# Oldest chunk first or youngest chunk first: the order of three chunks in each step of a chunked recurrence

## The chip, the cores and the metric

The kernel runs on one core of one Trainium2 chip. The metric is device time in microseconds (us). Engines: PE is the matrix engine, PEld its weight loads, DVE the vector engine, ACT the scalar engine, POOL the general one, SP the one that issues most transfers here.

## The reference, cut to what matters

The reference runs two transformer layers over a prompt of 512 tokens and a sample of 64. The change touches one piece of layer 0, the RWKV-7 token mixer: a matrix state per head (8 heads, 64 x 64) is carried from token to token,

```
def step(state, inp):
    r_t, w_t, k_t, v_t, a_t, bb_t = inp
    sa = jnp.einsum('bhij,bhj->bhi', state, a_t)
    state = state * w_t[:, :, None, :] + sa[..., None] * bb_t[:, :, None, :] + v_t[..., None] * k_t[:, :, None, :]
    return state, jnp.einsum('bhij,bhj->bhi', state, r_t)
```

and each head's output is then layer-normalised, given a bonus term and gated. The prompt starts from a zero state, the sample from a state that is an input.

## The kernel before, in words

The kernel does not go token by token. It cuts the 576 tokens into 9 chunks of 64 (chunk 8 is the sample) and writes each chunk's part of the recurrence as small matrix products, 64 x 64 blocks for 8 heads at a time. A chunk passes through 18 stages, `k` = 0 to 17:

- 0 and 1 make the products of keys and queries inside the chunk; 2 to 12 invert a triangular matrix by products and additions; none of these needs the state.
- 13, 14 and 15 are the chunk's turn on the carried state `ST`. Behind product 15, DVE adds to the state and scales it (L1217, L1218), and goes on with the layer norm of the output: mean, centred value, variance.
- 16 has no product: POOL takes the inverse root (L111), DVE scales the block with it (L1193).
- 17 turns the block back on PE (L1093); DVE applies gain and bias (L1232, four instructions) and adds and gates (L1239, L1240).

A stage is a group of products by PE into one or both PSUM banks of the chunk's lane, and then copies by ACT (L1179) or sums by DVE out of them. Only when these are done may PE begin the lane's next stage: it waits on the lane's signal `taken`. There are three lanes (own banks, own work tiles), and chunk `c` uses lane `c % 3`, so chunk `c + 3` starts in the lane that chunk `c` leaves.

Chunks start 6 steps apart (`LAG`). In step `tau`, chunk `c` is at stage `k = tau - 6 * c`, so in steps 12 to 53 three chunks are under way, at `r`, `r + 6` and `r + 12` with `r = tau % 6`. I call six such steps a round; there are seven. Chunk 8 has in addition, ahead of its own products from step 54 on, the first tile of the output projection (`first_tile`, L1262), which fills PE while few chunks are left.

Every engine's instructions run in the order in which the program lists them; a wait holds everything behind it on that engine. That order is the list `turns`, sorted by step. Within a step it goes by chunk, oldest first, with two exceptions that move output stages to the end of a step (17 on PE, 16 and 17 on DVE):

```
turns = [(tau, c, tau - LAG * c) for tau in range(LAG * last + NS) for c in range(NCH) if 0 <= tau - LAG * c < NS]
```

Which of DVE and ACT takes which stage: DVE takes 0, 1, 2 (four instructions, with a copy by ACT beside them), 4 (with ACT), 5 (with ACT), 7, 10, 11, 12, 15, 16, 17; ACT alone takes 3, 6, 8, 9, 13, 14.

Of the kernel before, what the change touches and what calls it, by code (L numbers as in the profile page):

```python
# [758 lines left out]
def rwkv(nc, io, sb, sig, bank, CST, BV, MIX, PC, lw, W2A, G2, IDN, wide, side, PA, PB, OC, OBT, X):  # L759
# [25 lines left out]
    with ExitStack() as s2:  # L785
# [28 lines left out]
        with nc.Block() as block:  # L814
            @block.gpsimd
            def _(pool):

                pool.wait_ge(cl.h, cl.at(16))
                for q in halves:
                    for dst, mask in ((MSI, maskSI.rearrange("p (a n) -> p a n", a=2)[q, :, q]), (M16, mask16[q, q]),  # L820
                                      (MO, maskO[q, q]), (M16L, mask16L[q, q])):
                        pool.tensor_copy(dst[q], mask).then_inc(mh.h, 1)
# [210 lines left out]
    with ExitStack() as s2:  # L1033
# [39 lines left out]
        def count(c, k):  # L1073

            return c // LANES * PRODUCTS + min(k, 16)
# [3 lines left out]
        turns = [(tau, c, tau - LAG * c) for tau in range(LAG * last + NS) for c in range(NCH) if 0 <= tau - LAG * c < NS]  # L1079
# [88 lines left out]
        def act_stage(act, c, k):  # L1168

            lane, w = c % LANES, work[c % LANES]  # L1170
            b = w.b
            copies = {2: [(w.Bt, v4(b[1]))], 3: [(w.D2, v4(b[0])), (w.D2T, v4(b[1]))], 4: [(w.D4T, v4(b[0]))],
                      5: [(w.D4, v4(b[0]))], 6: [(w.D8T, v4(b[0])), (w.Kt, v4(b[1]))],
                      8: [(w.WT, v4(b[1]))], 9: [(w.NT, v4(b[0]))],
                      13: [(TMP[:, :, :], v4(b[0]))], 14: [(SA, v4(b[1]))]}.get(k, [])
            if copies:
                act.wait_ge(made[lane].h, made[lane].at(count(c, k) + 1))
                for dst, src in copies:
                    ins = act.activation(dst, src, ACT.Copy)  # L1179
                ins.then_inc(taken[lane].h, 1 if k in (2, 4, 5) else 2)  # L1180
# [68 lines left out]
        def first_tile(pe, tau):  # L1249

            if tau == 54:
                for k in range(4):
                    m = pe.transpose(bank[6][:, k * P:(k + 1) * P], OC[:, 0, k * P:(k + 1) * P], ident)
                m.then_inc(ot.h, 1)
            for b, k in FIRST.get(tau, ()):
                if (b, k) == (0, 0):
                    pe.wait_ge(oc.h, oc.at(1))
                    pe.wait_ge(wl[0].h, wl[0].at(16))
                if (b, k) == (0, 4):
                    pe.wait_ge(wl[1].h, wl[1].at(32))  # L1260
                lhs = OCT[:, k * P:(k + 1) * P] if k < 4 else OBT[:, k - 4, 0:P]
                m = pe.matmul(bank[7 - b], lhs, first_out[k][:, b * 512:(b + 1) * 512], start=(k == 0), stop=(k == 7))  # L1262
                if k == 7:
                    m.then_inc(fo.h, 1)
# [3 lines left out]
        with nc.Block() as block:  # L1268
            @block.sync
            def _(sp):  # L1270
                wv = io["l0_w_out"].rearrange("(k p) n -> p k n", p=P)

                def through(c):
                    sp.wait_ge(made[c % LANES].h, made[c % LANES].at(count(c, 15) + 1))

                sp.dma_start(FO[:, 0:4, :], wv[:, 0:4, :]).then_inc(wl[0].h, 16)
                sp.dma_start(FO[:, 4:7, :], wv[:, 4:7, :]).then_inc(wl[1].h, 16)
                sp.dma_start(first_out[7], wv[:, 7, :]).then_inc(wl[1].h, 16)
                through(6)
                sp.dma_start(XF[:, 2560:3584], io["x_prompt"][0, 0:P, :]).then_inc(xf.h, 16)  # L1280
                sp.wait_ge(st_sig.h, st_sig.at(last))
                sp.dma_start(io["out_b_wkv_p"], ST[:, :, :]).then_inc(stored.h, 16)

                through(last - 1)
                sp.wait_ge(stored.h, stored.at(16))
                sp.dma_start(ST[:, :, :], io["wkv_t"]).then_inc(loaded.h, 16)
                sp.wait_ge(st_sig.h, st_sig.at(NCH))
                sp.dma_start(io["out_b_wkv_s"], ST[:, :, :]).then_inc(stored.h, 16)
                sp.wait_ge(stored.h, stored.at(32))

            @block.tensor
            def _(pe):
                for tau, c, k in sorted(turns, key=lambda turn: (turn[0], turn[2] == 17)):
                    if c == last:
                        first_tile(pe, tau)
                    pe_stage(pe, c, k)

            @block.scalar
            def _(act):
                for tau, c, k in turns:  # L1300
                    act_stage(act, c, k)
                    if (tau, c) == (55, last):
                        act.wait_ge(ot.h, ot.at(1))
                        act.activation(OCT, bank[6], ACT.Copy).then_inc(oc.h, 1)

            @block.gpsimd
            def _(pool):
                pool.memset(ST[:, :, :], 0.0).then_inc(zs.h, 1)
                pool.memset(OBT[:, :, TOK:PADT], 0.0).then_inc(zs.h, 1)
                for c in range(NCH):  # L1310
                    roots.give(pool, c, ys[:, 1, :])

            @block.vector
            def _(dve):
                ch = Chain(dve, dve_chain)
                for tau, c, k in sorted(turns, key=lambda turn: (turn[0], turn[2] > 15)):
                    if (c, k) == (0, 15):
                        dve.wait_ge(zs.h, zs.at(2))
                    if (c, k) == (last, 15):
                        dve.wait_ge(loaded.h, loaded.at(16))  # L1320
                    dve_stage(dve, ch, c, k)
                dve_chain.end(ch.n)
# [1497 lines left out]
```

## Time and profile before

| what | value |
|---|---|
| time, median of 3 runs | 3630.05 us (3628.56 to 3630.25) |
| the profiled execution's own time | 3630.2 us |
| its span | 3628.3 us |
| busy shares over the span | PE 83%, DVE 71%, ACT 37%, POOL 40% |
| the recurrence, first product to last gating | 328.0 to 503.6 us |
| three chunks under way, first to last full round's state update | 366.91 to 460.00 us |

In the timeline a product stands as two instructions, so the `x8` of the program's listing is `x16` there; the length shown for the last one reaches past the moment at which the next group may begin. The busy shares are means over a kernel of many stages; the recurrence is a twentieth of the span. Behind it comes the long part that gathers expert rows from memory.

### The profile page before, as it was taken

To read this page: it belongs to the slowest core of one execution; us is meant where nothing else is said; L and a number is where in the kernel's file an instruction comes from. 1 tells how busy PE (TensorE), PEld (TensorE's weight loads), DVE (VectorE), ACT (ScalarE), POOL (GpSimd) and SP (SyncE) were. 2 spreads that over 40 slices of the span, in tenths; PEclk is the share of its full clock that TensorE was granted. 3 is DMA by queue.
4 is the path that set the end of the run, shared out by engine and by line. 5 is a ranking of instruction groups with operands and counts; after the bars stand their busy time and mean duration, and the time that the engine had idled before them with its cause. 6 is when DMAs were issued, how large, how long until landed. Compare 5 with 4: busy or idle time off the path is not lost. (4 is left out here: it accounts for less than half of the span.)

```text
span 3628.3 us, 38367 instructions
## 1 busy us (share of the span) xinstructions
PE 3009.7 (83%) x11628; PEld 1431.6 (39%) x11628; DVE 2588.6 (71%) x6361; ACT 1343.5 (37%) x4033; POOL 1434.6 (40%) x1241
## 2 busy tenths in 40 slices
PE   8997969887777778999898788988988877777777
PEld 5774854342223223434344333433434322233222
DVE  2675648876666667798978577999777666666664
ACT  3354213333333333336653332345633333333332
POOL 1200014544444445454345454543444444444443
PEclk9997989999999999999998999999999999999999
DMA  4101049999999999999899999999999999999998
GB/s 134 39 15 48 4 164 420 412 419 408 422 421 421 401 421 396 419 410 389 330 413 403 393 415 419 420 411 344 416 421 421 414 413 420 421 421 406 422 421 352
DMA packets 216573, 1293.40 MB, mean 356 GB/s; under 512 B 23600, under 2 KB 41008, under 8 KB 68784
## 3 DMA queue, kind: packets, MB, share of 16 engines
q0 software_dynamic: 165888, 1208.03, 81.1%
q1 hardware_dynamic: 50480, 82.93, 6.5%
q8 instruction: 92, 1.51, 0.2%
q14 instruction: 113, 0.93, 0.1%
HBM read 1286.49 MB, written 3.87 MB: 356 GB/s over the span
## 5 line engine op out<-in xcount | busy, mean ns | idle before, releaser
L1592 PE MATMUL banks<-ring,route 128*128 128x512 f32 (+1 forms) x4184 | 2020.9, 620 | 525.7 <-ACT route L1577 504.0
L1500 POOL DMA_INDIRECT ring<-in_uv,route x1152 | 1326.3, 1151 | 1683.2 <-PE banks L1592 1541.1
L1511 DVE SCALAR_TENSOR_TENSOR ring<-ring,XN 128x1024 f32<-128x1024 f32 x1152 | 1423.4, 1236 | 742.7 <-DMA ring<-in_uv,route 732.6
L1592 PEld LDWEIGHTS banks<-ring,route 128*128 128x128 f32 (+1 forms) x4184 | 741.8, 188 | 1637.0 <-issue 857.3
L1562 ACT ACTIVATE route<-route 128x2 f32<-128x2 f32 x576 | 117.3, 204 | 1836.5 <-DVE ring L1511 1836.1
L1577 ACT ACTIVATE route<-IDN,route 128x128 f32<-128x128 f32 x918 | 317.0, 387 | 4.3 <-PE banks L1592 3.4
L1567 ACT ACTIVATE route<-route 128x1 f32<-128x1 f32 x1152 | 276.7, 287 | 23.1
L1920 PE MATMUL banks<-own,QP 128*128 128x512 f32 (+1 forms) x400 | 178.3, 570 | 4.1 <-ACT QP L2011 2.7
L1562 ACT ACT_TABLE_LOAD x106 | 136.0, 1283 | 1.9
L1521 DVE SCALAR_TENSOR_TENSOR X<-ring,route,X 128x1024 f32<-128x1024 f32 x106 | 135.7, 1280 | 0.0
L1920 PEld LDWEIGHTS banks<-own,QP 128*128 128x128 f32 x400 | 77.2, 194 | 94.2 <-issue 83.9
L1511 DVE DVE_READ_ACCUMULATOR ring<-ring,XN 128x1 f32 x1152 | 94.4, 82 | 0.0
L1408 ACT ACT_TABLE_LOAD x71 | 91.1, 1283 | 1.3
L1980 PE MATMUL banks<-own 128*128 128x320 f32 (+1 forms) x256 | 72.6, 425 | 3.9 <-DMA own<-in_l_peer_wq 3.9
L1972 PE MATMUL banks<-own,QP 128*128 128x512 f32 x160 | 75.2, 595 | 0.7 <-DMA own<-in_l_w_out 0.7
L111 POOL TENSOR_TENSOR ys<-ys,IDN 128x4 f32<-128x4 f32 x9 | 9.1, 1008 | 162.1 <-DVE ys L1228 162.1
L507 PE MATMUL banks<-XT,ring 128*128 128x288 f32 x288 | 71.8, 406 | 0.0
L111 POOL TENSOR_TENSOR hs<-hs,IDN 128x8 f32<-128x8 f32 x12 | 26.6, 2220 | 112.7 <-DVE hs L736 112.7
L1980 PEld LDWEIGHTS banks<-own 128*128 128x128 f32 x256 | 48.9, 196 | 37.7 <-issue 27.7
L507 PEld LDWEIGHTS banks<-XT,ring 128*128 128x128 f32 x288 | 54.6, 190 | 17.5 <-issue 2.4
L2403 PE MATMUL banks<-own 128*128 128x448 f32 x128 | 53.6, 545 | 0.0
L1467 DVE TENSOR_TENSOR route<-route 128x512 f32<-128x512 f32 x72 | 49.5, 687 | 0.0
(450 smaller groups left out, 3082.0 us busy)
## 6 DMA issues: line engine op xcount, KB each, us to landing
ring<-in_uv,route POOLq DMA_INDIRECT x1152
own<-in_l_w_in SPq DMA_DIRECT2D x16, 1024.0 KB
own<-in_l_w_out SPq DMA_DIRECT2D x12, 1024.0 KB
own<-in_l_peer_wq SPq DMA_DIRECT2D x12, 1024.0 KB
X<-in_x_prompt SPq DMA_DIRECT2D x8, 512.0 KB, 7.7
ring<-in_l_w_in SPq DMA_DIRECT2D x4, 1024.0 KB, 9.8
ring<-in_l_peer_wq SPq DMA_DIRECT2D x2, 2048.0 KB, 12.0
own<-in_l_w_in SPq DMA_DIRECT2D x4, 656.0 KB
```

Of the source, the lines that this page charges most:

```text
L507: m = pe.matmul(bank[(NT + i) % 2][:, 0:HALF], W[HOMES[s]][:, k, w], XT[:, k, HALF * half:HALF * half + HALF], start=(k == 0), stop=(k == ...
L1408: act.activation(self.GX, self.BS, ACT.Exp, bias=self.NM, accum_out=self.GS[:, 0:1]).then_inc(self.exped.h, 1)
L1500: pool.indirect_dma_start(self.ring[:, s % RING, :], None, self.io[f"uv{of_slot(s)[0]}"], bass.IndirectOffsetOnAxis(ap=self.EI[:, g % 2, k ...
L1511: dve.scalar_tensor_tensor(u, u, 1.0, self.XN[:, of_slot(s)[1], :], ALU.mult, ALU.mult, accum_out=self.HD[:, g % 2, k:k + 1]).then_inc(sel ...
L1521: dve.scalar_tensor_tensor(x, self.ring[:, s % RING, D:], self.WG[:, g % 2, k:k + 1], x, ALU.mult, ALU.add).then_inc(self.v_vector.h, 1)
L1562: act.activation(self.HG[:, par, k:k + 2], self.HD[:, par, k:k + 2], ACT.Gelu).then_inc(self.gelus.h, 1)
L1567: act.activation(self.WG[:, par, k + i:k + i + 1], self.HG[:, par, k + i:k + i + 1], ACT.Copy, scale=self.GT[:, g % 3, k + i:k + i + 1]).t ...
L1577: act.activation(self.DG[:, n % 4, 0:cols], on, ACT.Copy, scale=self.WG[:, par, k + i:k + i + 1]).then_inc(self.diagonals.h, 1)
L1592: m = pe.matmul(self.bank[1 + half][0:n, :], self.DG[:, (V_TENSOR[s] - 1) % 4, 0:n], self.ring[:, s % RING, D + 512 * half:D + 512 * half ...
L1920: m = pe.matmul(out[:, 0:W.shape[2]], self.QP[:, self.tiles[i], k, :], W[:, k % HK, :], start=(k == 0), stop=(k == KD - 1))
L1972: m = pe.matmul(out, self.QP[:, self.tiles[i], k, :], W[:, k % HK, :], start=(k == 0), stop=(k == KD - 1))
L1980: m = pe.matmul(out[:, 0:self.width()], W[:, k % HK, i * P:i * P + P], self.XQ[:, k, 0:self.width()], start=(k == 0), stop=(k == KD - 1))
```

## The change

Each of PE, ACT and DVE now sorts its turns by stage as well, so within a step the chunk with the lowest stage, the youngest, comes first. Output stages stay last on PE and DVE. No instruction is added or removed, no tile, bank, transfer or lane changes.

```diff
             @block.tensor
             def _(pe):
-                for tau, c, k in sorted(turns, key=lambda turn: (turn[0], turn[2] == 17)):
+                for tau, c, k in sorted(turns, key=lambda turn: (turn[0], turn[2] == 17, turn[2])):
                     if c == last:
                         first_tile(pe, tau)
                     pe_stage(pe, c, k)
 
             @block.scalar
             def _(act):
-                for tau, c, k in turns:
+                for tau, c, k in sorted(turns, key=lambda turn: (turn[0], turn[2])):
                     act_stage(act, c, k)
...
             @block.vector
             def _(dve):
                 ch = Chain(dve, dve_chain)
-                for tau, c, k in sorted(turns, key=lambda turn: (turn[0], turn[2] > 15)):
+                for tau, c, k in sorted(turns, key=lambda turn: (turn[0], turn[2] > 15, turn[2])):
```

Three places in the round in which chunk 2 is the oldest (lane 2, `banks2`), chunk 3 the middle one (lane 0, `banks0`) and chunk 4 the youngest (lane 1, `banks1`); chunk 5 then follows chunk 2 in lane 2.

The first place is PE from the last step of the round into the next round. Before, the rows are stages 11 and 5, then 17 of chunk 2, then 12 of chunk 3, 6 of chunk 4 (two rows) and 0 of chunk 5:

```order
L1087 MATMUL banks0<-PA 64x64 x8
L1087 MATMUL banks1<-PB 64x64 x16
L1093 MATMUL banks2<-CST,PB 64x64 x8
L1087 MATMUL banks0<-PA 64x64 x8
L1087 MATMUL banks1<-PB 64x64 x8
L1093 MATMUL banks1<-CST,ring 64x64 x8
L1108 MATMUL banks2<-ring,own 64x128 x8
```

After the change the same stretch of PE reads 5, 11, 17, then 0, 6 (two rows), 12:

```order
L1087 MATMUL banks1<-PB 64x64 x16
L1087 MATMUL banks0<-PA 64x64 x8
L1093 MATMUL banks2<-CST,PB 64x64 x8
L1108 MATMUL banks2<-ring,own 64x128 x8
L1087 MATMUL banks1<-PB 64x64 x8
L1093 MATMUL banks1<-CST,ring 64x64 x8
L1087 MATMUL banks0<-PA 64x64 x8
```

Stage 0 of the new chunk (L1108) now stands directly behind stage 17 of the chunk that leaves the same lane; the stages 12 and 6 that stood between them come behind it.

The second place is PE from step 2 of the round into step 3. Before, the rows are 14 of chunk 2 and 8 of chunk 3, then 2 of chunk 4 (two rows), then the first rows of 15 of chunk 2:

```order
L1087 MATMUL banks2<-ring,PB 64x64 x8
L1093 MATMUL banks0<-CST,PA 64x64 x8
L1087 MATMUL banks1<-own,ring 64x64 x8
L1093 MATMUL banks1<-CST,own 64x64 x8
L1154 MATMUL banks2<-PB 64x64 x2
L1156 MATMUL banks2<-ring,PB 64x64 x2
```

After the change they are 2 (two rows), 8, 14, then 3 of chunk 4, 9 of chunk 3, and the first row of 15:

```order
L1087 MATMUL banks1<-own,ring 64x64 x8
L1093 MATMUL banks1<-CST,own 64x64 x8
L1093 MATMUL banks0<-CST,PA 64x64 x8
L1087 MATMUL banks2<-ring,PB 64x64 x8
L1087 MATMUL banks1<-PB 64x64 x16
L1087 MATMUL banks0<-PA,X 64x64 x8
L1154 MATMUL banks2<-PB 64x64 x2
```

Between stages 2 and 3 of the youngest chunk there stood the whole of stage 15 and stage 9; now stages 8 and 14 stand there.

The third place is PE behind stage 15. Before, the last row of 15 is followed by 9 and 3 of its own step, then by 10, 4 and 11:

```order
L1162 MATMUL banks2<-ring,PB 64x64 x2
L1087 MATMUL banks0<-PA,X 64x64 x8
L1087 MATMUL banks1<-PB 64x64 x16
L1087 MATMUL banks0<-PA 64x64 x8
L1087 MATMUL banks1<-PB 64x64 x16
L1087 MATMUL banks0<-PA 64x64 x8
```

After the change the last row of 15 is followed by 4 and 10, and then by 5 and 11:

```order
L1162 MATMUL banks2<-ring,PB 64x64 x2
L1087 MATMUL banks1<-PB 64x64 x16
L1087 MATMUL banks0<-PA 64x64 x8
L1087 MATMUL banks1<-PB 64x64 x16
L1087 MATMUL banks0<-PA 64x64 x8
```

Stages 9 and 3 have moved ahead of 15. On DVE the whole of 15 still comes ahead of the sums of 10 and 4, and these two have changed places.

## Rows read from the trace of the kernel before

**Rows 1.** Windows, two stretches of the recurrence: stretch, busy time by engine, granted clock, DMA, GB/s.

```profile
328.00:340.00 12.00, 7.89 (x96) 6.74 (x96) 3.08 (x6) 0.77 (x3) 0.56 (x2) 0.50 0.91 345
400.00:420.00 20.00, 18.66 (x569) 17.80 (x571) 14.38 (x38) 4.77 (x13) 2.02 (x2) 1.00 0.02 4
```

**Rows 2.** Timeline of DVE, the first state update with three chunks and the last.

```profile
366.91 0.42 DVE L1217 TENSOR_TENSOR STr<-banks,STr 128x256 f32<-128x256 f32 x1 [0.60 <-PE banks L1162]
...
460.00 0.42 DVE L1217 TENSOR_TENSOR STr<-banks,STr 128x256 f32<-128x256 f32 x1 [0.53 <-PE banks L1162]
```

**Rows 3.** Timeline of PE in one round: start, length, operation, count, [idle before <- releaser].

```profile
392.51 1.04 PE L1108 MATMUL banks<-ring 64*64 64x128 f32 x16
393.38 0.63 PE L1087 MATMUL banks<-ring,PB 64*64 64x64 f32 x16
...
394.93 0.63 PE L1093 MATMUL banks<-CST,own 64*64 64x64 f32 x16
395.39 0.28 PE L1154 MATMUL banks<-PB 64*64 64x64 f32 x4
...
397.73 0.63 PE L1087 MATMUL banks<-PA,X 64*64 64x64 f32 x16
398.19 1.10 PE L1087 MATMUL banks<-PB 64*64 64x64 f32 x32
399.13 0.63 PE L1087 MATMUL banks<-PA 64*64 64x64 f32 x16
400.05 1.15 PE L1087 MATMUL banks<-PB 64*64 64x64 f32 x32 [0.29 <-ACT PB L1179]
401.40 0.68 PE L1087 MATMUL banks<-PA 64*64 64x64 f32 x16 [0.20 <-DVE PA L1213]
...
402.85 0.63 PE L1093 MATMUL banks<-CST,PB 64*64 64x64 f32 x16
403.31 0.63 PE L1087 MATMUL banks<-PA 64*64 64x64 f32 x16
...
404.25 0.63 PE L1093 MATMUL banks<-CST,ring 64*64 64x64 f32 x16
405.14 1.09 PE L1108 MATMUL banks<-ring,own 64*64 64x128 f32 x16 [0.26 <-DVE PB L1232]
406.57 0.33 PE L1145 MATMUL banks<-STr,ring 64*64 64x64 f32 x4 [0.34 <-DVE PA L1215]
```

**Rows 4.** Timeline of DVE in the same round.

```profile
395.61 0.43 DVE L1202 TENSOR_TENSOR PB<-PB,own 128x256 f32<-128x256 f32 x1 [1.25 <-PE banks L1093]
...
396.99 0.43 DVE L1205 TENSOR_TENSOR PB<-banks,own 128x256 f32<-128x256 f32 x1
397.94 0.42 DVE L1217 TENSOR_TENSOR STr<-banks,STr 128x256 f32<-128x256 f32 x1 [0.53 <-PE banks L1162]
...
402.13 0.42 DVE L1193 TENSOR_TENSOR PB<-PB,ys 128x256 f32<-128x256 f32 x1 [0.46 <-POOL ys L111]
...
403.53 1.55 DVE L1232 TENSOR_SCALAR PB<-banks,BV 128x64 f32<-128x64 f32 x4
```

**Rows 5.** Timeline of PE in the later part: two waits for ACT.

```profile
1514.55 3.64 PE L1592 MATMUL banks<-ring,route 128*128 128x512 f32 x4 [1.91 <-ACT route L1577]
...
3399.65 2.84 PE L1592 MATMUL banks<-ring,route 128*128 128x512 f32 x6 [2.23 <-ACT route L1577]
```

**Rows 6.** Windows behind these waits, columns as in rows 1.

```profile
1514.50:1515.00 0.50, 0.45 (x1) 0.37 (x2) 0.00 (x0) 0.00 (x0) 0.44 (x1) 0.73 1.03 422
...
1518.00:1518.50 0.50, 0.50 (x3) 0.41 (x2) 0.26 (x2) 0.00 (x0) 0.03 (x1) 0.86 0.94 385
...
3402.00:3403.00 1.00, 1.00 (x4) 0.28 (x2) 0.71 (x1) 0.00 (x0) 0.84 (x1) 1.00 1.05 434
```

**Rows 7.** Timeline of SP and PE where the next part begins.

```profile
504.42 0.43 SPq L2542 DMA_DIRECT2D ring<-in_l_peer_wq  x1
...
514.94 1.40 PE L2614 MATMUL banks<-XN,ring 128*128 128x128 f32 x5 [2.70 <-DMA ring<-in_l_peer_wq]
```

## The prediction

> **What bounds the kernel now.** I read three views. The windows come first, to see which engine fills the recurrence: with three chunks under way PE is busy 18.66 of 20 us, DVE 14.38, ACT 4.77, at the full granted clock, and almost nothing is transferred [rows 1]. So PE's queue sets the pace, and what counts is the time in which PE stands still. Next the state updates on DVE, which give the length of a round: from 366.91 to 460.00 are six rounds, 15.51 us each [rows 2]. Last the timeline of PE and DVE in one round, to see where PE stands still and for whom [rows 3, 4].
>
> In rows 3 the time between the starts of two groups is what a group costs. A group of 8 products takes 0.46 us (402.85 to 403.31), a two-bank group of 16 takes 0.94 (398.19 to 399.13), a group with 128 columns 0.87 (392.51 to 393.38). What a start comes later than that is a stall. There are four in a round:
>
> - stage 0 at 405.14: 0.89 behind the group ahead of it, so a stall of 0.43. It waits for the four L1232 of the chunk that leaves its lane.
> - stage 13 at 406.57: 1.43 − 0.87 = 0.56. It waits for stage 12's sum, which on DVE stood behind L1239 and L1240.
> - stage 4 at 400.05: 0.92 − 0.46 = 0.46. It waits for ACT's two copies of stage 3.
> - stage 11 at 401.40: 1.35 − 0.94 = 0.41. It waits for stage 10's sum, which stood behind all of stage 15 on DVE.
>
> That is 1.86 us of 15.51. The carried state is not what sets the round: a state update starts at 397.94, and the next chunk's stage 13 takes it up at 406.57 [rows 3, 4]. Bringing the oldest chunk forward or back is therefore worth nothing in itself; only the cover behind each wait counts.
>
> **The change part by part.** Nothing is added or removed; the work of a round, 15.51 − 1.86 = 13.65 us of PE, stays. For each lane I ask how long its engine needs before the lane's next stage may begin, and what PE has to do meanwhile. From the end of a group's issue DVE starts 0.22 us later (394.93 + 0.46 = 395.39 to 395.61), and PE starts 0.06 us behind DVE's end (403.53 + 1.55 = 405.08 to 405.14) [rows 3, 4].
>
> First place, **stage 17 and stage 0 of one lane**. PE's 17 takes 0.46, DVE then needs 0.22 + 1.55 + 0.06 = 1.83 before stage 0 may start. Before, 12 and 6 lay between (0.46 + two groups of 0.46) and left 0.43 exposed. Now nothing lies between: PE stands still for 1.83, and behind it wait 6, 12 and all that follows. L1239 and L1240 now run beside stage 0's products (0.87 + 0.22 before DVE could use them), so they delay nothing. This meets chunks 3 to 8: six times.
>
> Second place, **stage 2 to stage 3 of the youngest**. DVE's four instructions run from 395.61 to 396.99 + 0.43 = 397.42; with the start and the way back 0.22 + 1.81 + 0.06 = 2.09 [rows 4]. Before, stages 15 and 9 covered it fully. Now 8 and 14 do, 0.92: a stall of 1.17, in each of seven rounds. 9 and 15 are late behind it.
>
> Third place, **behind stage 15**. From the end of its issue at 397.73 to the start that follows DVE's first free sum, 401.40, are 3.67 us [rows 3]. Before, 9, 3, 10 and 4 covered all but the stalls 0.46 and 0.41. Now DVE takes stage 4's sum first, an instruction of the same length, and PE has only 4 and 10 to do, 0.94 + 0.46 = 1.40: a stall of 2.27, seven times. 5, 11 and 17 wait behind it. Stage 17 itself also needs POOL's root and L1193, done at 402.13 + 0.42, 4.82 behind the end of 15's issue; PE comes to it at 3.67 + 0.94 + 0.46 = 5.07, so this stays hidden by 0.25 us, and costs at most that little if I am off.
>
> What goes away: stage 0's 0.43 six times, and the 0.56 (12 and 13 now have 1 and 7 between them, 0.87 + 0.46), the 0.46 (stage 15's 2.33 us now cover ACT's copies of 3) and the 0.41 seven times each. ACT's own order moves with PE's and nothing waits on it at either end: its work is 4.77 of 20 us [rows 1].
>
> The sum: 6 × 1.83 + 7 × (1.17 + 2.27) = 35.1 us come, 6 × 0.43 + 7 × (0.56 + 0.46 + 0.41) = 12.6 go, net 22.5 us. A full round becomes 15.51 − 1.86 + 5.27 = 18.9 us. Steps 0 to 11 and 54 to 65 get no term: with one or two chunks the two orders differ little, and at the end the first tile's products fill PE. Nothing behind the recurrence takes the delay up: the next part's first weights are asked for at 504.42, after the recurrence's end at 503.6, and PE waits for them at 514.94 [rows 7]; so the whole amount reaches the end.
>
> **The clock** is the part that no row of this stretch shows. At the third place PE now idles 2.27, does 1.86 of work (5, 11, 17) and idles 1.83 again; as the timeline counts idle time (the last product reaches 0.17 past its group's cost) these are 2.1 and 1.66. Elsewhere in this trace an idle time of 1.91 was followed by a fall of the granted clock, while one of 2.23 was not [rows 5, 6]. The fall: 0.73 in the half microsecond from 1514.50 means from about 1514.73; 0.86 in that from 1518.00 means until about 1518.14. That is 3.4 us at 1.2 instead of 2.4 GHz, so some 1.7 us lost where PE is the bound, as it is behind the first place (0, 6, 12, 1, 7, 13 follow without a stall). The bounds are nothing and one fall in each round, 7 × 1.7 = 11.9 us. Two waits close together, of lengths between which the rows are divided, make me take three falls in seven rounds: 5.1 us.
>
> The Trainium skill speaks against the change more strongly here: TensorE: Matmul & The Clock Gate, section "HAM oscillation — how this bites in real kernels", tells of bursts of products between waits that begin at the low clock each time and pay for it each time. By that rule the sum would be 22.5 + 11.9. The trace agrees with it at 1514.55 and not at 3399.65.
>
> **Rivals.**
> - The clock holds: 3630.2 + 22.5 = 3652.7. For it: rows 5's 2.23. 30%.
> - The clock falls in some rounds, the forecast: 3630.2 + 22.5 + 5.1 = 3657.8. 40%.
> - It falls in every round (this is the skill's rule): 3630.2 + 34.4 = 3664.6; twice in some, up to 3676. 15%.
> - PE stays at the low clock throughout, as from 328 to 340, when one chunk alone kept it busy 7.89 of 12 us at 0.50 [rows 1]: 13.65 us of work a round doubled is 27.3, and 7 × 11.8 make 3713. Against it: 6.6 us of unbroken work follow each first place. 3%.
> - The largest new wait is covered by something I don't see, say DVE doing stage 4's sum ahead of the layer norm's tail: then 7 × 2.27 fall out, and 3637 is left. Against it: the listing puts the sum behind all of 15, and DVE takes its instructions in order throughout rows 4. 6%.
> - Faster: only the four old stalls count. It would need the three waits (1.83, 2.09, 3.67) to be over before PE is through with the work that covers them (0, 0.92, 1.40), that is, from new stalls under 1.86 a round on the sign turns. With none of them 3630.2 − 12.6 = 3617.6. For it speaks that every lane still has two others to hide behind in a cycle of three; against it, that stage 15, the one long piece of PE, now stands beside two lanes whose waits are already over. 4%.
> - No change, because a later wait for a transfer takes the delay up: 3630. Rows 7 show no transfer under way that could. 2%.
>
> **How the numbers follow.** The forecast is the likeliest case, 3658 us; the profiled execution of before (3630.2) stands 0.15 us above the median of the runs, so I correct nothing. The range holds the first three cases but not the doubled falls: from 3645 (the 22.5 with a third of it wrong) to 3670 (a fall in each round and some 5 us more). Anything beyond 0.2%, 7.3 us, is about what a measurement can tell from no change. Slower takes the first five cases, 0.94; faster 0.04; within the bound 0.02.
>
> **What the changed profile would show.** The state updates on DVE 18.9 us apart, or up to 20.6 where the clock fell. Before stage 0 (L1108) an idle time of about 1.7 us released by L1232; before stage 3 about 1.0 released by L1205; before stage 5 about 2.1 released by L1207, the sum of stage 4. No wait of stage 13 for L1215, none of stage 4 for ACT. PE busy about 72% of these 20 us. The clock at 1.00, with dips to 0.50 of some 3.4 us behind the pair of waits. The recurrence would end near 531, and everything behind it would look as before. It would be wrong if updates stayed near 15.5 us apart, or if one of the three releasers were another engine.

## The result

| | before | changed |
|---|---|---|
| time, median of 4 runs each | 3629.31 us (3625.33 to 3630.25) | 3658.66 us (3657.25 to 3659.22) |
| ratio, 95% interval | | 1.008 (1.0069 to 1.0092) |
| the profiled execution's own time, span | 3630.2, 3628.3 us | 3659.11, 3657.2 us |
| recurrence, start of the first product to end of the last L1240 | 175.5 us | 206.2 us |
| one round, mean of six | 15.52 us | 20.37 us |

The change makes the kernel 29 us slower; the forecast was 3658 (3645 to 3670). The total is right and its two terms are not: the profile after and the first run below show that the stalls brought less than 22.5 us and the clock more than 5.1.

The windows of the changed kernel, for the stretches of [rows 1]: PE was busy 18.66 of the 20 us from 400, and is now busy 15.28; the granted clock, 1.00 before, has a mean of 0.91.

```profile
328.00:340.00 12.00, 7.63 (x96) 6.45 (x93) 3.08 (x6) 1.04 (x3) 0.26 (x2) 0.50 0.90 349
400.00:420.00 20.00, 15.28 (x436) 14.81 (x434) 10.78 (x27) 3.90 (x11) 1.01 (x1) 0.91 0.01 3
```

DVE's state updates of the changed kernel, at the start and the end of six rounds as in [rows 2], are 122.22 us apart, against 93.09 before.

```profile
367.58 0.42 DVE L1217 TENSOR_TENSOR STr<-banks,STr 128x256 f32<-128x256 f32 x1 [4.12 <-PE banks L1162]
...
489.80 0.42 DVE L1217 TENSOR_TENSOR STr<-banks,STr 128x256 f32<-128x256 f32 x1 [4.05 <-PE banks L1162]
```

PE's timeline in one round of the changed kernel, for [rows 3]:

```profile
402.56 0.63 PE L1087 MATMUL banks<-ring,PB 64*64 64x64 f32 x16
404.17 1.15 PE L1087 MATMUL banks<-PB 64*64 64x64 f32 x32 [0.97 <-DVE PB L1205]
...
408.88 0.63 PE L1087 MATMUL banks<-PA 64*64 64x64 f32 x16
411.61 1.68 PE L1087 MATMUL banks<-PB 64*64 64x64 f32 x32 [2.09 <-DVE PB L1207]
413.08 1.06 PE L1087 MATMUL banks<-PA 64*64 64x64 f32 x16
413.94 1.06 PE L1093 MATMUL banks<-CST,PB 64*64 64x64 f32 x16
416.66 1.09 PE L1108 MATMUL banks<-ring,own 64*64 64x128 f32 x16 [1.66 <-DVE PB L1232]
```

All three new stalls are there, with the releasers and the lengths that were forecast: stage 3 waits for stage 2 on DVE (404.17 − 402.56 − 0.46 = 1.15 us), stage 5 for stage 4's sum behind all of 15 (411.61 − 408.88 − 0.46 = 2.27), stage 0 for L1232 of the chunk that leaves its lane. What wasn't forecast stands between the last two: from the start of stage 11 to that of stage 17 it is 0.86 us, not 0.46. DVE's timeline has stage 4's sum (L1207), which starts at 411.14 behind the layer norm, and L1232, which reads stage 17:

```profile
411.14 0.42 DVE L1207 TENSOR_TENSOR PB<-banks,PB 128x256 f32<-128x256 f32 x1
...
415.05 1.55 DVE L1232 TENSOR_SCALAR PB<-banks,BV 128x64 f32<-128x64 f32 x4 [0.36 <-PE banks L1093]
```

The windows of the changed kernel around these stages, columns as in [rows 1], the granted clock last but two:

```profile
411.00:411.50 0.50, 0.00 (x0) 0.00 (x0) 0.47 (x4) 0.00 (x0) 0.19 (x1) 1.00 0.00 0
411.50:412.00 0.50, 0.39 (x12) 0.39 (x14) 0.39 (x2) 0.00 (x0) 0.50 (x1) 0.99 0.00 0
412.00:412.50 0.50, 0.50 (x16) 0.50 (x14) 0.15 (x1) 0.00 (x0) 0.32 (x1) 0.50 0.00 0
...
415.00:415.50 0.50, 0.00 (x1) 0.00 (x0) 0.41 (x2) 0.00 (x0) 0.00 (x0) 0.59 0.07 16
```

From about 411.99 to 415.41 PE has 1.2 instead of 2.4 GHz. By such windows the clock fell in each of the seven rounds (once for 6.8 us, else 3.4), each time right behind the stall that follows stage 15. The old stalls are gone: in the list of waits of PE in these rounds neither L1215 nor L1213 nor ACT's L1179 is left as a releaser, and stage 0's idle 0.26 [rows 3] has become the 1.66 above.

What follows the recurrence is only later [rows 7]: the weights asked for at 504.42 are now asked for at 534.79, and PE's first product with them starts 30.9 us later:

```profile
545.85 1.41 PE L2614 MATMUL banks<-XN,ring 128*128 128x128 f32 x5 [3.23 <-DMA ring<-in_l_peer_wq]
```

The whole execution is 28.9 us longer, so some 2 us come back in the 3100 us behind. Runs of before differ among themselves by more (3626 to 3633), and I didn't follow it.

### The profile page after: what moved, and what is told of

It reads as the page before. It is cut to its first block and busy times, and to the rows that moved or that the text cites. A ratio compares the mean times of both kernels' runs of the same rounds, so it can differ in the third digit from the quotient of the medians.

```text
span 3657.2 us, 38367 instructions
## 1 busy us (share of the span) xinstructions
PE 3022.9 (83%) x11628; PEld 1444.5 (39%) x11628; DVE 2586.2 (71%) x6361; ACT 1342.6 (37%) x4033; POOL 1439.3 (39%) x1241
## 5 line engine op out<-in xcount | busy, mean ns | idle before, releaser
L1087 PE MATMUL banks<-PB 64*64 64x64 f32 x1152 | 46.9, 235 | 17.5 <-DVE PB L1207 10.5
L1179 ACT ACTIVATE PB<-banks 128x256 f32<-128x256 f32 x63 | 22.6, 383 | 85.2 <-PE banks L1087 50.2
```

## The experiments

All ten in one table; the ratio is given where a kernel was timed in several runs, the rest were run once. "Length" and "round" are those of the first table, each from one profiled execution.

| run | time, us | ratio (95%) | length, us | round, us | clock in the rounds |
|---|---|---|---|---|---|
| e1_filled | 3648.2 | 1.005 (1.0035 to 1.0065) | 195.7 | 18.78 | 1.00 |
| e2_young_early | 3636.4 | 1.002 (1.001 to 1.0029) | 183.3 | 16.96 | 1.00 |
| e3_young_late | 3665.6 | 1.0096 (1.008 to 1.0111) | 214.4 | 20.57 | falls in each |
| e4_middle_first | 3626.9 | 0.9991 (0.9982 to 1.0001) | 173.6 | 15.05 | 1.00 |
| e5_act_old | 3662.7 | | 211.3 | 20.58 | falls in each |
| e6_young_end | 3625.0 | | 175.3 | 15.52 | 1.00 |
| e7_filled_lane | 3662.0 | | 207.7 | 20.30 | falls in each |
| e8_middle_end | 3627.4 | 0.9993 (0.9984 to 1.0002) | 172.7 | 15.05 | 1.00 |
| e9_half_filled | 3646.3 | | 195.3 | 18.79 | 1.00 |
| e10_filled_inverse | 3658.1 | | 206.0 | 20.34 | falls in each |

**The stalls without the clock.** The first run fills the longest stall of the changed kernel with products whose results nobody uses:

```diff
                     pe_stage(pe, c, k)
+                    if k == 10 and 12 <= tau < 54:
+                        for _ in range(2):
+                            pe.matmul(bank[6][:, :], ident, CST[:, 0:512], start=True, stop=True)
```

> The changed kernel with two extra products (128x512, into a bank that lies idle until step 54) on PE behind stage 10 in steps 12 to 53; their results are not used. By rows of the first tile two such products take 1.9 us, so they lie inside the stall of 2.27 behind stage 15 and shift nothing. Theory (the low clock behind that stall costs about 1.4 us a round on top of the stalls): the granted clock stays at 1.00, a round is 18.9 us instead of 20.4, the recurrence ends some 9 to 10 us earlier than in the changed kernel, the time is about 3649. Rival (the extra 1.4 us a round are not the clock, or the second stall of 1.66 drops it all the same): the round stays at 20.1 to 20.4, time 3657 to 3660. Third case: the extra products delay stages 5 and 11, and the time is above 3660.

PE does more work and the kernel is 10.5 us faster than the changed one. In its timeline of PE the extra products (L1299) lie in the stall, and stage 0 still waits, by 413.30 − 411.01 − 0.46 = 1.83 us (1.66 as idle time):

```profile
407.40 1.98 PE L1299 MATMUL banks<-CST,IDN 128*128 128x512 f32 x4
409.56 1.15 PE L1087 MATMUL banks<-PB 64*64 64x64 f32 x32 [0.18 <-DVE PB L1207]
...
411.01 0.63 PE L1093 MATMUL banks<-CST,PB 64*64 64x64 f32 x16
413.30 1.09 PE L1108 MATMUL banks<-ring,own 64*64 64x128 f32 x16 [1.66 <-DVE PB L1232]
```

Its windows show that the clock doesn't fall:

```profile
400.00:420.00 20.00, 17.12 (x476) 15.34 (x472) 11.63 (x30) 4.66 (x13) 1.01 (x1) 1.00 0.01 4
```

Its state updates, in DVE's timeline, are 112.66 us apart over six rounds:

```profile
368.56 0.42 DVE L1217 TENSOR_TENSOR STr<-banks,STr 128x256 f32<-128x256 f32 x1 [4.12 <-PE banks L1162]
...
481.22 0.42 DVE L1217 TENSOR_TENSOR STr<-banks,STr 128x256 f32<-128x256 f32 x1 [4.05 <-PE banks L1162]
```

So the two terms are parted. With the clock up the recurrence is 195.7 − 175.5 = 20.2 us longer than before: that is the stalls. The other 206.2 − 195.7 = 10.5 us are the clock, 1.5 a round.

**Each half of the round alone.** Both runs sort as below, with `turn[0] % 6 < 3` (e2) or `turn[0] % 6 > 2` (e3) as the condition `young`:

```diff
-                for tau, c, k in sorted(turns, key=lambda turn: (turn[0], turn[2] == 17)):
+                for tau, c, k in sorted(turns, key=lambda turn: (turn[0], turn[2] == 17, turn[2] if young else -turn[2])):
...
```

> Youngest first only in steps 0 to 2 of a round; steps 3 to 5 keep the order of before. Theory (a sum of covers): stage 0 directly behind 17 stalls 1.83 (before 0.43), stage 15 now comes directly behind stage 14 of its own lane and waits for ACT's copy, about 0.7, stage 13's 0.56 goes, those of 4 and 11 stay; a round of 15.51 + 1.40 + 0.7 - 0.56 = 17.1, time 3630 + 6 x 1.40 + 7 x 0.15 = 3639 to 3641 if the clock holds with a single idle time of 1.7 a round. Rival (any such wait drops the clock once a round): some 7 to 10 us more, 3647 to 3650.

The round is 16.96 us; the terms of the sum make 17.05, not 17.1. The clock holds. The time is 3 us under what was expected; the first update comes 1.25 us earlier behind the first product than before, and the rounds make under 1 of it. The timeline shows stage 0's stall and the one that this mixture adds, stage 15 (L1154) waiting for ACT's copy of 14:

```profile
406.73 1.09 PE L1108 MATMUL banks<-ring,own 64*64 64x128 f32 x16 [1.66 <-DVE PB L1232]
...
413.90 0.33 PE L1154 MATMUL banks<-PB,X 64*64 64x64 f32 x4 [0.54 <-ACT PB L1179]
```

> Youngest first only in steps 3 to 5; steps 0 to 2 keep the order of before. Theory: stage 3 comes directly behind stage 2 of its own lane, a stall of 2.09 us; behind stage 15 the stall of 2.27 is there as in the changed kernel; stages 4's 0.46 and 11's 0.41 go, 0's and 13's stay; a round of 15.51 + 2.09 + 2.27 - 0.87 = 19.0 with the full clock, time 3630 + 7 x 3.49 = 3654. The two idle times lie 5 us apart here, not 1.9. If it is the pair close together that drops the clock, it stays at 1.00 and the time is 3654; if the one idle time of 2.1 behind stage 15 does it, the clock falls in every round as in the changed kernel and the time is 3661 to 3666.

A round is 20.57 us: the 19.0 of the sum and 1.6 more, which I put down to the clock; no run has this order with the clock up. It falls, though no two of the long idle times stand close together (6.9 and 9.7 us lie between them), so the prediction's picture of a pair is not needed. But it doesn't fall where I expected either. Of the 38.9 us by which the recurrence is longer than before, 8.2 lie ahead of the first update; I didn't split them. Its timeline of PE, the idle 2.09 behind stage 15 and the 1.90 ahead of stage 3:

```profile
399.61 0.68 PE L1087 MATMUL banks<-PA 64*64 64x64 f32 x16 [2.09 <-DVE PA L1207]
...
411.18 1.15 PE L1087 MATMUL banks<-PB 64*64 64x64 f32 x32 [1.90 <-DVE PB L1205]
```

Its windows behind the one and the other: the first leaves the clock at 1.00, the second is followed by the fall.

```profile
400.00:400.50 0.50, 0.50 (x24) 0.50 (x22) 0.15 (x1) 0.00 (x0) 0.31 (x1) 1.00 0.00 0
...
412.00:412.50 0.50, 0.50 (x22) 0.50 (x20) 0.00 (x0) 0.12 (x1) 0.00 (x0) 0.83 0.00 0
```

**Which idle time drops the clock.** Three more kernels fill one stall each of the changed kernel, by products like those of the first run: behind stage 17 (e7: 512 and 384 columns), half of the one behind stage 15 (e9: 512 columns behind stage 10), and the one ahead of stage 3 (e10: 512 columns behind stage 14).

```diff
                     pe_stage(pe, c, k)
+                    if k == 14 and 12 <= tau < 54:
+                        pe.matmul(bank[6][:, 0:512], ident, CST[:, 0:512], start=True, stop=True)
```

> The changed kernel with two extra products (128x512 and 128x384, results not used) behind stage 17, in the stall ahead of stage 0; the stall behind stage 15 stays open. Theory (the idle time of 2.1 behind stage 15 is what drops the clock, with or without the one ahead of stage 0): the clock still falls to 0.50 in every round right behind it; stage 17 and the extra products then run at half rate and overrun their stall by about 1.5 us, round 20 to 22 us, time 3660 to 3672. Rival (the prediction's: the two idle times 1.9 apart drop it together): the clock stays at 1.00, the extra products (some 1.7 us at full rate) fit into the stall of 1.83, round 18.9, time about 3649.

> The changed kernel with one extra product (128x512, result not used) behind stage 10, which leaves some 1.2 us of the idle time behind stage 15 open; the idle times of 1.66 ahead of stage 0 and 0.97 ahead of stage 3 stay. Theory (an idle time of 2.1 there is what drops the clock, and 1.66 does not, as in the run with youngest first only in steps 0 to 2): clock at 1.00, round 18.8, time about 3649. Rival (the sum of the three idle times in a round decides, now about 3.8 instead of 4.7): the clock still falls in some rounds, which are then 20 us long, time 3653 to 3659.

> The changed kernel with one extra product (128x512, result not used) behind stage 14, which fills the idle time of 0.97 ahead of stage 3; those of 2.1 behind stage 15 and 1.66 ahead of stage 0 stay. Theory (the 2.1 behind stage 15 decides): the clock falls in every round, rounds of 20.1 to 20.4, time 3656 to 3662. Rival (idle time over the whole stretch from stage 2 to stage 5 decides, so that less of it ahead keeps the clock up): clock at 1.00, round 18.8, time about 3649.

With stage 0's stall filled (e7) the idle 2.1 stands as it was, by the timeline of PE:

```profile
410.19 1.80 PE L1087 MATMUL banks<-PB 64*64 64x64 f32 x32 [2.10 <-DVE PB L1207]
```

and the windows behind it show that the clock falls all the same:

```profile
410.50:411.00 0.50, 0.50 (x16) 0.50 (x14) 0.07 (x1) 0.00 (x0) 0.39 (x1) 0.50 0.00 0
```

With stage 3's filled (e10) the idle 2.1 stands, too, by the timeline:

```profile
412.71 1.79 PE L1087 MATMUL banks<-PB 64*64 64x64 f32 x32 [2.10 <-DVE PB L1207]
```

and the windows:

```profile
413.00:413.50 0.50, 0.50 (x16) 0.50 (x14) 0.05 (x1) 0.00 (x0) 0.42 (x1) 0.50 0.00 0
```

With half of the one behind stage 15 filled (e9) the timeline has 1.04 idle left:

```profile
407.88 1.15 PE L1087 MATMUL banks<-PB 64*64 64x64 f32 x32 [1.04 <-DVE PB L1207]
```

The clock then holds, by the windows, and the round is that of the full filling:

```profile
400.00:420.00 20.00, 15.89 (x460) 14.72 (x462) 11.15 (x28) 3.89 (x11) 1.01 (x1) 1.00 0.01 3
```

In the changed kernel, then, the idle 2.1 behind stage 15 is the cause, and neither of its neighbours is needed by itself; idle times of 1.66 and 0.97 drop nothing. Nor is it the sum of the idle times: e7 leaves 2.10 + 0.97 = 3.07 us of them in a round and the clock falls, e9 leaves 1.04 + 1.66 + 0.97 = 3.67 and it holds. Length alone isn't the rule, as e3 shows. In e7 the extra products overran their stall by less than 0.1 us, not by the 1.5 that I expected.

**ACT's order.** The changed kernel with the line of ACT as it was:

> The changed kernel with ACT's order of before; PE and DVE as changed. Theory of the prediction (ACT's order decides nothing, ACT is busy a fifth of the time and each of its copies has cover): rounds as in the changed kernel, 20.1 to 20.4 us, time 3656 to 3662. A sum of covers in finer steps says a little more: in step 2 ACT then copies 14 and 8 ahead of stage 2's block, done about 0.2 us after DVE's four instructions, so stage 3 starts 0.2 later and a round is 0.2 longer. Rival (the orders of PE and ACT must agree, or PE stands still for copies): a stall released by ACT of 0.5 us or more in each round, time above 3663.

The time lies between the two. In its list of waits (total, times, longest) stage 3 now waits for ACT, up to 1.1 us, where it waited 0.97 for DVE:

```profile
PE banks L1087 <- ACT PB L1179: 6.9, 7, 1.1
```

By the letter this is the rival's sign, a stall of over 0.5 us released by ACT, but it stands in the place of one that was there. A round is 0.2 longer; one of them has the low clock for 6.8 us, as in the changed kernel. In this one run the whole recurrence is 5 us longer: 2 ahead of the first update, 1.3 in the rounds, the rest behind them. So ACT's order is worth tenths of a microsecond in a round, a little more than the nothing that the prediction gave it, and it adds no stall of 0.5.

**The last steps.** The condition `young` is now `turn[0] > 53`:

> The order of before up to step 53, youngest first only in steps 54 to 65, where chunks 7 and 8 are left and the first tile fills PE. The prediction gave these steps no term; in the changed kernel the two intervals from the seventh state update on hold some 1.6 us less than its stalls and its clock make up. Theory (the new order gives this back there, since stage 9 of the last chunk and the first tile's products stand ahead of stage 15 instead of behind it): rounds of 15.5, and the recurrence ends 1 to 2 us earlier than the 503.6 of before, time 3628 to 3630. Rival (these steps are bound by PE and its work is the same): it ends at 503.6 within 0.5.

The recurrence ends at 500.96, but it also begins 2.4 us earlier than before. Its length is 175.3 against 175.5, so the rival holds in this run. From the seventh update to the end it takes 43.26 us against 43.55. By the windows the clock falls once more in this stretch, 5.6 us ahead of the end here and 2.6 us in the kernel before, so the order alone may be worth a little more.

**A version that is not slower.** The sums of covers point to a gain, too: what covers stage 12's sum is too short in the order of before. The diff is e4's line for PE; ACT and DVE sort alike. e8 adds youngest first from step 54 on.

```diff
-                for tau, c, k in sorted(turns, key=lambda turn: (turn[0], turn[2] == 17)):
+                for tau, c, k in sorted(turns, key=lambda turn: (turn[0], turn[2] == 17, (turn[0] % 6 < 2 and turn[2] // 6 != 1))):
...
```

> The kernel before with the middle chunk ahead of the oldest in steps 0 and 1 of a round: stage 6 ahead of 12, and 7 ahead of 13; all else as before. Theory: the cover of stage 12's sum grows by stage 7's 0.46, so stage 13's stall of 0.56 shrinks to about 0.1, and the others stay: a round of 15.0 to 15.1 instead of 15.51, 7 x 0.46 = 3 us, time about 3627, which is less than 0.2% and shows in the round length of the trace rather than in the time. Rival (stage 1 or 2 of the youngest waits in its place, since 0 now stands nearer to 1): round 15.5, time 3630.

> Middle chunk first in steps 0 and 1 of a round (rounds of 15.05 us by the last run of it), and youngest first from step 54 on. Theory (two small gains that add): rounds of 15.05, the stretch from the seventh state update to the end 0.3 to 0.7 us shorter than the 43.55 of before, recurrence 173 us long against 175.5, time 3626 to 3627, with the upper end of the interval below that of before. Rival (the end's order is worth nothing): recurrence 173.6, time 3627.

The round falls to 15.05 us in both, and in the rounds PE's waits for L1215 are gone, as summed. The first and the last update of six rounds of e4, in DVE's timeline:

```profile
367.63 0.42 DVE L1217 TENSOR_TENSOR STr<-banks,STr 128x256 f32<-128x256 f32 x1 [0.60 <-PE banks L1162]
...
457.91 0.42 DVE L1217 TENSOR_TENSOR STr<-banks,STr 128x256 f32<-128x256 f32 x1 [0.53 <-PE banks L1162]
```

Behind the seventh update e8 takes 43.08 us, 0.47 less than before, as its theory says, though its clock falls 3.2 us ahead of the end. Of the time neither interval excludes 1: 2.6 and 2.9 us under the medians of before are about what the runs can't tell, and the clear gain in time that I expected of e8 isn't shown. What is shown is the shorter round.

## Why the prediction was right

- **What bounds the kernel, and the three places**: right. Places, releasers and lengths were 1.83, 1.17 and 2.27 forecast, and 1.83 (first run), 1.15 and 2.27 measured. The old stalls went.
- **The sum of the stalls, 22.5**: 20.2 with the clock up. The round is 18.78, not 18.92, which makes 0.9 in six rounds. The rest, about 1.4, lies ahead of the first update and behind the last full one: I counted a seventh round in full and gave the last steps no term. The runs with the new order of the last steps show 0.3 (e6) and 0.47 (e8) of it; the rest stays open.
- **The clock, three falls of 1.7 us**: the step that failed. The clock fell in all seven rounds, and at another place: not behind the pair of stalls, into a stretch without stalls, but behind the first of the two, into stages 5, 11 and 17. There it costs 1.4 (DVE reads stage 17 at 415.05; 411.61 + 0.94 + 0.46 + 0.46 + 0.22 = 413.69 at full clock), 10.5 us in all with the one double fall. So the rival "in every round" is what happened, a little cheaper than its 11.9. The forecast's reason for three falls, the pair of waits, is not it: in e7 the pair is gone and the clock falls in all seven rounds. The Trainium skill's TensorE: Matmul & The Clock Gate, section "HAM oscillation — how this bites in real kernels", tells of bursts that each begin at the low clock behind a wait for a transfer. Those waits are longer than the ones here, which the prediction left out when it took the section for a fall in every round. The trace has that outcome, the low clock from 0.0 to 0.8 us behind the start of stage 5 in each of the seven rounds, at a shorter wait.
- **The total**: 22.5 + 5.1 = 27.6 forecast, 20.2 + 10.5 = 30.7 in the recurrence. The two errors went opposite ways, and 2 us came back behind it. The mechanism of the stalls was right and that of the clock was not; that the figure is within 1 us of 3658.66 is luck.
- **The rivals of the other side** didn't show: no wait was over before its cover, and nothing took the delay up.

## What to carry to other kernels

In an in-order pipeline of several lanes, write down for each stage how long the lane needs until its next stage may start, and what the engine has to do meanwhile in the listed order; the difference is the stall, and here it was right to 0.02 us for the three new ones, from one round of the kernel before. Turning a cyclic order round doesn't keep the cover, since the stages are unequal: here the 2.33 us of stage 15 covered the 2.09 behind stage 2, and after the change 0.92 of work was left there. And price a new stall on PE with the clock, too: here 20 us of stalls brought 10.5 us more.

## What the runs showed of the hardware

I hadn't expected that filling an idle engine with useless products could be worth 10.5 us, nor that half the filling (1.04 us of 2.1 left idle; one run) is worth as much as the whole. The granted clock fell in every round behind idle times of 2.1 (changed kernel, e5, e7, e10) and 1.90 (e3), and held behind 1.66 (e1, e2, e9), but also behind 2.09 in e3 and 2.23 elsewhere [rows 5, 6]; what tells these apart wasn't settled.

One thing in the windows bears on it. In the changed kernel the falls begin at 371.03, 391.52, 411.99, 432.47, 452.95, 473.44 and 493.92: 20.48 us apart, though the rounds take 20.1 to 21.1 us. In e3, e5, e7 and e10 the falls in the rounds are 20.48 us apart, too. So a fall doesn't come at a fixed moment behind its stall. Why the falls keep this spacing, and whether it tells the cases above apart, wasn't tested. All five kernels have rounds of 20.3 to 20.6 us on average, so the seven falls in seven rounds, and with them the 10.5 us, are shown for such rounds only.
